# Logit products of a layer's head pairs: the two heads' half-array products issued in turn, the mask products of both behind them

## The reference, cut to what matters

```python
def stick_breaking_attention(q, k, v):
    ...
        z = jnp.einsum('bqhd,bshd->bhqs', qb, k).astype(jnp.float32) * scale
        strict = key_pos[None, :] < t[:, None]
        log_rest = jnp.where(strict, jax.nn.log_sigmoid(-z), 0.0)
        tail = lax.cumsum(log_rest, axis=3, reverse=True) - log_rest
        a = jnp.where(strict, jnp.exp(jax.nn.log_sigmoid(z) + tail), 0.0)
        return jnp.einsum('bhqs,bshd->bqhd', a.astype(v.dtype), v)

def dsa_sparse_attention(q, k, v, q_idx, k_idx, w_idx, rel_bias, topk):
    ...
        vals, idx = lax.top_k(score, topk)
        ...
        logits = jnp.einsum('bqhd,bqkhd->bqhk', qb, kg).astype(jnp.float32) * scale
        ...
        p = jax.nn.softmax(logits, axis=-1)
        return jnp.einsum('bqhk,bqkhd->bqhd', p.astype(vg.dtype), vg)
```

## Time and profile before

| | |
|---|---|
| median of 3 runs | 3016.38 us (3012.67 to 3020.07) |
| the profiled execution | 3014.64 us, of which the span from first to last instruction is 3012.9 us |
| PE matmuls | 2428.3 us busy (81%), 9721 passes |
| DVE | 1743.7 us busy (58%) |
| ACT | 905.9 us busy (30%) |
| POOL | 979.0 us busy (32%) |
| mean granted clock of TensorE | 0.888 of full speed |
| DMA | 803.85 MB, mean 267 GB/s |

### The profile page before, as it was taken

One profiled execution on the slowest core, in us unless ns is written; L12 is line 12 of the kernel. 1 busy time (PEld: TensorE's weight loads), 2 busy tenths in 40 slices (PEclk: granted clock), 3 DMA queues, 4 the chain that ended last, 5 costly groups with the idle time before them and its releaser, 6 DMA issues. The chain is left out here.

```text
span 3012.9 us, 30208 instructions
## 1 busy us (share of the span) xinstructions
PE 2428.3 (81%) x9721; PEld 1627.9 (54%) x9721; DVE 1743.7 (58%) x3652; ACT 905.9 (30%) x1730; POOL 979.0 (32%) x691
## 2 busy tenths in 40 slices
PE   6997999869876888889785996798557468559897
PEld 4776878758653343334333664575246336436674
DVE  3444311031128888988964687587669859855142
ACT  4444222223311222222222442244134324323232
POOL 2232554433302434343451234234213523410001
PEclk9998999979988999999897997898778677769899
DMA  4321333223118999999998899899789999964553
GB/s 159 94 66 49 98 105 97 101 71 108 56 39 330 392 418 409 411 412 403 403 416 351 320 366 369 331 355 402 277 342 382 413 400 373 390 269 157 215 185 138
DMA packets 255851, 803.85 MB, mean 267 GB/s; under 512 B 18302, under 2 KB 138518, under 8 KB 190183
## 3 DMA queue, kind: packets, MB, share of 16 engines
q0 software_dynamic: 73728, 536.90, 43.9%
q1 hardware_dynamic: 181991, 265.35, 25.3%
HBM read 793.36 MB, written 14.07 MB: 268 GB/s over the span
## 5 line engine op out<-in xcount | busy, mean ns | idle before, releaser
L1335 POOL DMA_INDIRECT gathered<-in_peer_rows,experts x436 | 530.6, 1217 | 928.8 <-DVE x_res L2452 630.7
L1446 PE MATMUL peer_banks<-gathered,peer_diags 128*128 128x512 f32 x720 | 342.8, 633 | 60.3 <-ACT peer_diags L1506 60.2
L78 PE MATMUL group_banks<-group_x_t,group_ring 128*128 128x128 f32 (+1 forms) x2016 | 340.2, 332 | 15.9 <-ACT group_x_t L2264 8.4
L2438 DVE CUSTOM_DVE_ANT_0 gathered<-gathered,late_nat 128x1024 f32<-128x1024 f32 x256 | 315.7, 1236 | 42.0 <-DMA gathered<-in_peer_rows,experts 29.0
L78 PEld LDWEIGHTS group_banks<-group_x_t,group_ring 128*128 128x128 f32 x2016 | 307.6, 208 | 46.0 <-ACT group_x_t L2264 10.8
L2452 DVE SCALAR_TENSOR_TENSOR x_res<-gathered,group_weights,x_res 128x1024 f32<-128x1024 f32 x256 | 329.8, 1288 | 2.5
L1446 PEld LDWEIGHTS peer_banks<-gathered,peer_diags 128*128 128x128 f32 x720 | 144.6, 204 | 249.5 <-issue 249.2
L2082 PE MATMUL group_banks<-group_ring,group_x_t 128*128 128x512 f32 x512 | 233.3, 610 | 28.2 <-DMA group_ring<-in_weights 28.2
L1609 DVE CUSTOM_DVE_ANT_0 peer_product<-gathered,early_nat 128x1024 f32<-128x1024 f32 x180 | 214.8, 1222 | 41.2 <-DMA gathered<-in_peer_rows,experts 41.1
L1446 PE MATMUL peer_banks<-peer_early_gathered,peer_diags 128*128 128x512 f32 x304 | 148.9, 643 | 45.9 <-ACT peer_diags L1506 45.9
L1499 ACT ACTIVATE peer_acts<-peer_dots 128x2 f32<-128x2 f32 x128 | 26.0, 203 | 518.1 <-DVE peer_dots L1609 517.9
(11 more groups left out here) (324 smaller groups left out, 4307.9 us busy)
## 6 DMA issues: line engine op xcount, KB each, us to landing
group_ring<-in_weights SPq DMA_DIRECT2D x270, 512.0 KB, 5.5
mixer_wq<-in_w_in SPq DMA_DIRECT2D x24, 512.0 KB, 4.4
mixer_wk<-in_w_in SPq DMA_DIRECT2D x24, 512.0 KB, 5.7
peer_w<-in_w_pq SPq DMA_DIRECT2D x8, 1024.0 KB
gathered<-in_peer_rows,experts POOLq DMA_INDIRECT x436
diff_wv<-in_w_in SPq DMA_DIRECT2D x8, 512.0 KB, 4.2
conv_wb<-in_w_in SPq DMA_DIRECT2D x8, 512.0 KB, 4.1
merge_w<-in_w_conv_out SPq DMA_DIRECT2D x8, 512.0 KB, 3.6
```

What stands on the lines that cost most here:

```text
L78: last = nc.tensor.matmul(out, lhsT, rhs, start=n == 0, stop=n == len(pairs) - 1)
L1335: nc.gpsimd.indirect_dma_start(row_buffer(m, r), None, A["peer_rows"], bass.IndirectOffsetOnAxis(ap=at, axis=0))\
L1446: last = nc.tensor.matmul(ps[:, ACC[unit % 2] + half, :], diags[:, r % DIAGS, :], row_buffer(m, r)[:, D + half * BANK:D + (half + 1) * BAN ...
L2438: nc.vector.tensor_tensor_reduce(out=row, in0=row, in1=m.late_nat[:, t % 2, :], scale=1.0, scalar=0.0, op0=ALU.mult, op1=ALU.add, accum_ou ...
```

## The change

In `stick_logits` the loop over the two heads becomes the inner one: for each tile of keys the product of head 0 and that of head 1 are issued one behind the other, and the mask products of both heads follow behind all of them. In `sparse_logits` the loops over heads and tiles change places too. Banks, operands, semaphores and the number of instructions stay.

```diff
+                    def bank(e):
+                        return ps[:, pair_banks(u) + e, :]
+
+                    for i in range(last + 1):
+                        t = max(i, first)
+                        at, width = lay.stick[i, t], (last - t + 1) * P
+                        for e in range(2):
+                            rows = slice(e * DH, (e + 1) * DH)
+                            nc.tensor.matmul(bank(e)[:, at:at + width], k_t[rows, n % 3, i * P:(i + 1) * P], q_t[rows, n % 2, (t - first) * P:NQ],
+                                             start=i == 0, stop=False, skip_group_check=True)
                     for e in range(2):
-                        bank, rows = ps[:, pair_banks(u) + e, :], slice(e * DH, (e + 1) * DH)
-                        for i in range(last + 1):
-                            t = max(i, first)
-                            at, width = lay.stick[i, t], (last - t + 1) * P
-                            nc.tensor.matmul(bank[:, at:at + width], k_t[rows, n % 3, i * P:(i + 1) * P], q_t[rows, n % 2, (t - first) * P:NQ],
-                                             start=i == 0, stop=False, skip_group_check=True)
                         for t in tiles:
                             at = lay.stick[t, t]
-                            made = nc.tensor.matmul(bank[:, at:at + P], m.ident[:, :], m.not_before[:, :], start=False, stop=False, skip_group_check=True)
+                            made = nc.tensor.matmul(bank(e)[:, at:at + P], m.ident[:, :], m.not_before[:, :], start=False, stop=False, skip_group_check=True)
                     made.then_inc(logits_done, 1)
...
-                    for e in range(2):
-                        rows = slice(e * DH, (e + 1) * DH)
-                        for t in tiles:
+                    for t in tiles:
+                        for e in range(2):
+                            rows = slice(e * DH, (e + 1) * DH)
                             made = nc.tensor.matmul(ps[:, pair_banks(u) + e, lay.row[t]:lay.row[t] + ROW_W[t]], q_t[rows, n % 2, local(t)],
                                                     k_t[rows, n % 3, 0:ROW_W[t]], start=True, stop=True)
```

## The result

| | before | after |
|---|---|---|
| median | 3018.2 us (6 runs, 3012.67 to 3022.36) | 2999.47 us (6 runs, 2989.41 to 3008.89) |
| ratio to before | | 0.9942, 95% interval 0.9925 to 0.9959 |
| the profiled execution | 3014.64 us, span 3012.9 | 2989.41 us, span 2987.6 |
| PE matmuls busy | 2428.3 us | 2399.5 us |
| mean granted clock | 0.888 | 0.889 |

The change makes the kernel faster by 0.58%: 17.5 us of 3018.2, and between 12.4 and 22.6 by the interval. The forecast was 2999 us and a gain of 15.9. The runs of one kernel spread over 10 us before and 20 after, and the profiled execution happens to be the lowest of its six. So the 25.3 us between the two spans is more than the change brings, and I compare distances within the trace, not places.

The account below looks back on a forecast made before the run. PE was taken as the bound in the last group, DVE's ordered background rows as what counts in the first. Gains of 10.2 + 4.1 + 1.6 = 15.9 us from 3014.64 gave 2999 us; eight-in-ten range 2991 to 3008.

Parts of the forecast that it names:

- The price of a block: One `stick_logits` on PE: 1.64 us for 2.91 in the last group, 1.42 for 2.47 in the second, 1.85 for 2.88 in the first.
- The last group's 10.2 us: Stick phase of the last group: all of the 1.27 us saved per block lies on the path, 8 blocks, 10.2 us.
- ACT's reserve: ACT's idle time before each softplus in the last group: 1.98 us, of which 0.7 us would be left.
- The first group's 4.1 us: First group's stick phase: DVE's waits at pairs 0 and 1 each give 1.03 us, 4.1 of 8.2 us.
- pairs 2 and 3 give nothing: First group: DVE comes later than these pairs' logits, so PE's gain there only lengthens PE's wait in the sparse phase.
- The second group's 1.6 us: Second group's stick phase: DVE's waits at one pair per layer give 1.05 and 0.6, together 1.6 of 8.4 us.
- The sparse part's 0: Swapped loops of `sparse_logits`: 0 us, since the first group's halves already run side by side; bound 0.2 us in all.
- The first two groups give nothing: Rival: late DMA rows and PE's clock falling after longer idling leave only the last group's 10.2 us; 3004.4 us, chance 0.14.
- The idle time itself: PE's wait at the head of the first group's sparse phase, forecast to grow by about 2 us in each layer.
- No overlap among many small products: Rival: in `stick_logits` only the mask's place counts, 0.3 us a block, 4 us in all; 3010.5 us, chance 0.06.
- Slower: Rival: the array runs empty at each change of half, so last-group blocks take 3.9 us for 2.91; 3029 us, chance 0.04.

## Why the prediction was right

**The price of a block** held in all three groups: 1.64, 1.42 and 1.85 us at full clock, to the hundredth. That the halves run side by side was read from the sparse logits, and the run with both heads on one half shows that it is the halves and not the neighbourhood.

**The last group's 10.2 us** were 5.1 in each layer's trace, and 9.7 us (3.0 to 16.3) in the run with this group alone. ACT's reserve shrank to the 0.7 us that were named.

**The first group's 4.1 us** stand in the traces: DVE is 2.07 us nearer to the first logits behind the second pair, in each layer. That pairs 2 and 3 give nothing is shown by the run without them. But the split that the prediction gave was wrong. It had each of two waits give 1.03 us because each was longer than that, and it left out ACT, which stands between the logits and DVE. In the second layer the waits went from 1.7 and 6.8 us to 1.4 and 5.0, that is by 0.3 and 1.8. ACT's softplus of the first pair there, before, then with the change:

```profile
1963.47 0.81 ACT L2313 ACTIVATE group_work<-group_banks 128x768 f32<-128x768 f32 x1 [0.32 <-PE group_banks L2114]
```

```profile
1959.07 0.81 ACT L2317 ACTIVATE group_work<-group_banks 128x768 f32<-128x768 f32 x1
```

ACT was busy with a gelu of the background work until 0.32 us before the logits came, so the first pair's logits could give 0.3 us and no more. The rest was not lost, since PE ran on without waiting for DVE and brought the second pair's logits 2.07 us earlier. So the sum came out as forecast because PE carried the first block's gain on to the second pair, where DVE waits again, a step that the prediction did not have. In the first layer the same happened, but the first wait is longer than before (6.7 for 5.4 us). It is 6.9 in the kernel with the last group alone, with the old loops there, so it varies without the change.

**The second group's 1.6 us** were right in the sum and wrong in both terms. The wait in the first layer fell from 4.5 to 2.7 us, by 1.8 and not by 1.05: that block ran in part at the lower clock before (mean 0.75) and took 3.18 us, where it takes 1.42 now. The wait of 0.6 in the second layer is still 0.6, where the forecast had counted all of it. There ACT came from a gelu straight into the softplus, without idle time, before and after. That 1.8 and 0 add up to about 1.6 is luck. The run with the first two groups alone gave 5.7 us, as 4.1 + 1.6 said, but with an interval from 0.3 to 10.9 it can't tell these terms apart.

**The sparse part's 0** held. On this point the Trainium skill's page "TensorE: Matmul & The Clock Gate", section "Part 3: Packing small matmuls — row/col tiling", which has matmuls start in strict program order, was weighed against the row and set aside; two runs bear that out, the one with the old sparse loops and the one in which head 1 begins while three passes of head 0 are still to come.

**The rivals.** "The first two groups give nothing" named a cost that did appear: in the first layer the longer idle time at the head of the sparse phase now ends in a stretch at half clock (1.65 us for 0.93). But the kernel with the last group alone has it too, with the old loops there (1.65 us behind 4.11 us of idle time), so it isn't tied to the change. How much it takes back was not separated by a run. The idle time itself was to grow by about 2 us and grew by 3.0 and 1.1. "No overlap among many small products" would have come true in part if the heads had not been taken in turn: with more than four passes of one half ahead, the other half begins late. "Slower" is excluded: a change of half costs no 0.07 us, since sixteen passes that go to and fro between the halves take 1.09 us, as eight passes without any did.

**The whole.** 15.9 us were forecast and 17.5 measured (12.4 to 22.6). The difference is within the interval, and no cause is sought for it. The main mechanism, the halves side by side and the last group's whole gain on the path, is shown; the 5.7 us of the first two groups came out with the wrong split.

## What to carry to other kernels

Products that use half of the array's rows should be issued in turn between the halves, with everything that uses all rows put before or behind the whole set. Here that halved the time of the half-array products. The gain counts in full where PE is the bound. Elsewhere it counts only where the engine at the end of the chain really waits, and only as far as the engine between them (here ACT) is idle when the products end: look at that engine's idle time too, before a wait is counted as gain. To price such an order, look for a place in the same trace where the two halves already meet without a full-array product between. And before a loop is reordered for a shorter period, add up the idle time of its bounding engine over the whole phase: with 1.1 us of it in each layer, no order could have brought four in all.

## What the runs showed of the hardware

- A pass of the lower half can overtake passes of the upper half that stand before it in the program: behind four it began 0.01 us late, behind six 0.33, behind eight 0.555, always with three passes of the other half still to come. Passes of 128 columns on one half kept their distance of 0.11 us from each other.
- Two halves at once slow neither: eight passes of 128 columns on one half take 1.09 us to the next full-array pass, weight loads included, whether or not eight passes of the other half run beside them.
- A mask product in rounded fp32 is one pass, and to put such passes behind plain fp32 ones cost nothing extra: it is 1.09 us to the first mask with them as without them.
- Runs of one unchanged kernel differ by 10 to 20 us. In the two traces compared here 4.5 us of difference stand in one stretch that the change left alone: 1.5 us are idle time of PE, and about 3 go with a granted clock that averaged 0.74 in one and 0.93 in the other.
